# Starting the merge's first product one tile at a time, with the last gate chunk and the turning of the attention outputs moved around it

## The chip, the cores and the metric

The kernel runs on one core of a Trainium2 chip, as one launch. The metric is the time of a launch in device microseconds (us); the number used is the median of several runs. The engines are named as in the profile: PE is TensorE's matmul pipe and PEld its weight loads, DVE is VectorE, ACT is ScalarE, POOL is GpSimd and SP is SyncE, which issues most DMAs.

## The reference, cut to what matters

The model is two layers of FFN, token mixing and FFN, then one hybrid layer with attention and a mixture of experts. Sequence 256, width 1024, fp32. The change touches the end of the attention and the start of what follows it, the merge:

```python
# token_mix, each of the two layers; o_a and o_b are 256x512
g_a, g_b = jnp.split(g_merge, 2, axis=-1)
y = jax.nn.sigmoid(g_a) * (o_a @ w_branch_a) + jax.nn.sigmoid(g_b) * (o_b @ w_branch_b)
return y @ w_out
# hybrid_layer, once; y_a comes from a convolution, y_b from attention
merged = jax.nn.sigmoid(gate_conv_l) * p_a + jax.nn.sigmoid(gate_attn_l) * p_b
x = x + gate1[:, None, :] * (merged @ w_o)
```

## The kernel before

Every weight is streamed from HBM in blocks of 128x2048 fp32 (1 MB), three blocks to a unit. SP loads block r of the next unit into `raw` once DVE has taken the old one apart (`load_stream`, L421). ACT rounds each block to `w_hi` in two halves (`split`, L506) when it has landed and PE has freed the place (`used`); DVE then writes the rest, `w_lo` (L945). Every large product is three matmuls (`mm3`, L1754 to L1756): high times high, low times high, high times low. Activations that are a left operand are split the same way after PE has turned (transposed) them into PSUM.

The order of the work is written out by hand, a list for each engine, and each engine takes its own list strictly in order; semaphores hold the lists together. In the attention, `jobs_run` walks 12 jobs in each of the two layers (`JOBS`) and 4 in the hybrid layer (`HYB_JOBS`). A job is one kind of attention, one tile of 128 queries and 4 heads. In step j PE issues the scores of job j+1, then `beside(j)`, then the turning of job j's probabilities (L1995, behind ACT's four Exp of that job, L614), then P times V of job j-1 (L1977). PV of the last job comes behind the loop. ACT copies the turned probabilities out (L624) and DVE scales each P times V output into `o_a`, `o_b` or `o_h` (`job_out`, L1202 and L1212), which gives PSUM bank 6 free for the next P times V (`o_done`).

`beside(j)` holds work that has nothing to do with the attention. On PE it is a chunk of the product for the merge's gates: two or three of 24 row blocks of the four gate sets in the layers, half a set in the hybrid layer, into banks 2 and 3. On ACT it is the `w_hi` half of a block split, and, where a set is finished, its two Sigmoids out of banks 2 and 3 (L729, hybrid L761). On DVE it is the `w_lo` half of that split.

Behind the jobs PE turns the outputs `o_a` and `o_b` (two groups of 4 transposes each, L2005), ACT rounds them (L738), DVE takes the rest (L1428). In the hybrid layer only `o_h`, the right-hand product's operand, is turned here (ACT L826, DVE L1564); the left-hand one comes from the convolution and is there earlier. Then `merge`: the first half is the product with the first branch's weights, 4 chunks for each of two token tiles, tile 0 into banks 0 and 1, tile 1 into banks 2 and 3 (`half_product`); a tile ends with a one-column matmul (`release`, L1735) which tells DVE that it is done. DVE multiplies it by the gate (L1150, `ya_done`), and the second half, with the second branch's weights into the same banks, waits for that tile by tile. The merge uses three weight units: the first half reads blocks 0 and 1 of the first, the second half block 2 of it and block 0 of the next.

```python
jobs_run(l * NJ, l * 6, JOBS, beside)                       # PE, L2165
pe.wait_ge(w_evac_a, l * 9 + 9)
pe.wait_ge(o_done, l * NJ + NJ)
for b in range(4):
    o = o_a if b < 2 else o_b
    ...
merge(u_mix + MIX_IN_UNITS, l, True)
```

## Time and profile before

| what | us |
|---|---|
| median of 3 runs | 1853.35 |
| lowest and highest of them | 1852.48, 1854.16 |
| the profiled execution's own time | 1855.78 |
| its span in the profile | 1854.1 |

| engine | busy us | share of the span |
|---|---|---|
| PE | 1764.3 | 95% |
| PEld | 1427.1 | 77% |
| DVE | 1376.3 | 74% |
| ACT | 957.9 | 52% |
| POOL | 46.9 | 3% |

Busy time on PE is the sum of pipelined matmuls and says only where it stood still, not that it ran at its peak. The chain that ended last is followed back from the last instruction; its shares say which engine set the time. All times below are us from the start of the span, in the one profiled execution.

### The profile page before, as it was taken

To read this page: it belongs to the slowest core of one execution; us is meant where nothing else is said; L and a number is where in the kernel's file an instruction comes from. 1 tells how busy PE (TensorE), PEld (TensorE's weight loads), DVE (VectorE), ACT (ScalarE), POOL (GpSimd) and SP (SyncE) were. 2 spreads that over 40 slices of the span, in tenths; PEclk is the share of its full clock that TensorE was granted. 3 is DMA by queue.
4 is the path that set the end of the run, shared out by engine and by line. 5 is a ranking of instruction groups with operands and counts; after the bars stand their busy time and mean duration, and the time that the engine had idled before them with its cause. 6 is when DMAs were issued, how large, how long until landed. Compare 5 with 4: busy or idle time off the path is not lost.

```text
span 1854.1 us, 24899 instructions
## 1 busy us (share of the span) xinstructions
PE 1764.3 (95%) x8645; PEld 1427.1 (77%) x8645; DVE 1376.3 (74%) x2097; ACT 957.9 (52%) x1433; POOL 46.9 (3%) x92
## 2 busy tenths in 40 slices
PE   5999999999999999999999999999899897999998
PEld 3788778787788878886878777887687775888876
DVE  6887676766876578777677578775776477999997
ACT  3444354664544454445437554444434546777775
POOL 0000000000000000000000000000000000000000
PEclk8999999999999999999989999999998998999999
DMA  8988743134576758884612338986562533999994
GB/s 361 359 324 301 287 172 136 69 127 169 204 280 257 255 187 336 316 305 174 248 69 92 135 138 311 343 302 245 189 253 93 203 136 114 363 347 375 347 350 166
DMA packets 61802, 437.43 MB, mean 236 GB/s; under 512 B 6816, under 2 KB 7328, under 8 KB 9504
## 3 DMA queue, kind: packets, MB, share of 16 engines
q1 hardware_dynamic: 47504, 339.27, 48.6%
q0 software_dynamic: 12672, 92.28, 13.4%
q10 hardware_dynamic: 1552, 4.89, 0.8%
q8 instruction: 47, 0.77, 0.2%
q14 instruction: 27, 0.22, 0.0%
HBM read 435.36 MB, written 1.05 MB: 235 GB/s over the span
## 4 chain that ended last, share of the span: by engine, by line
PE 82%; DVE 11%; ACT 4%; issue 2%; DMA 1%; ACTq 0%; SPq 0%; DVEq 0%; POOLq 0%
PE bank L1754 24%; PE bank L1755 24%; PE bank L1756 24%; DVE w_lo L945 2%; PE bank L1977 2%; DVE ada_w L969 1%; ACT w_hi L506 1%; PE bank L1995 1%; DMA ada_w<-ada_pairs 1%; PE bank L1836 1%; PE bank L1957 1%; DVE arena L1243 1%; PE bank L2005 1%; PE bank L1955 1%; PE bank L2297 1%
## 5 line engine op out<-in xcount | busy, mean ns | idle before, releaser
L945 DVE TENSOR_TENSOR w_lo<-raw,w_hi 128x1024 fp32r<-128x1024 f32 x426 | 501.5, 1220 | 223.2 <-ACT w_hi L506 222.9
L506 ACT ACTIVATE w_hi<-raw 128x1024 fp32r<-128x1024 f32 x426 | 426.5, 1053 | 363.3 <-PE bank L1756 359.2
L1754 PE MATMUL bank<-w_hi,uT_hi 128*128 128x512 f32 (+3 forms) x1424 | 558.4, 392 | 20.3 <-DVE uT_lo L1260 12.6
L1755 PE MATMUL bank<-w_lo,uT_hi 128*128 128x512 f32 (+3 forms) x1424 | 543.9, 382 | 0.0
L1756 PE MATMUL bank<-w_hi,uT_lo 128*128 128x512 f32 (+3 forms) x1424 | 543.4, 382 | 0.0
L1754 PEld LDWEIGHTS bank<-w_hi,uT_hi 128*128 128x128 f32 x1424 | 271.5, 191 | 80.1 <-DVE uT_lo L1260 14.0
L1756 PEld LDWEIGHTS bank<-w_hi,uT_lo 128*128 128x128 f32 x1424 | 270.7, 190 | 52.1
L1755 PEld LDWEIGHTS bank<-w_lo,uT_hi 128*128 128x128 f32 x1424 | 271.6, 191 | 48.6 <-issue 1.4
L1754 PE MATMUL bank<-w_hi,r_arena 128*128 128x512 f32 (+1 forms) x744 | 299.1, 402 | 6.2 <-DVE r_arena L1652 2.3
L1755 PE MATMUL bank<-w_lo,r_arena 128*128 128x512 f32 (+1 forms) x744 | 295.1, 397 | 0.0
L1756 PE MATMUL bank<-w_hi,r_arena 128*128 128x512 f32 (+1 forms) x744 | 292.6, 393 | 0.0
L969 DVE CUSTOM_DVE_ANT_0 ada_w<-ada_w,cmpw 128x1024 f32<-128x1024 f32 x176 | 206.9, 1218 | 5.9 <-DMA ada_w<-ada_pairs 5.9
L1754 PEld LDWEIGHTS bank<-w_hi,r_arena 128*128 128x128 f32 x744 | 140.8, 189 | 42.0 <-DVE r_arena L1652 3.0
L1756 PEld LDWEIGHTS bank<-w_hi,r_arena 128*128 128x128 f32 x744 | 140.4, 189 | 32.9
L1755 PEld LDWEIGHTS bank<-w_lo,r_arena 128*128 128x128 f32 x744 | 140.8, 189 | 30.1
L952 DVE TENSOR_TENSOR w_lo<-raw,w_hi 128x1024 fp32r<-128x1024 f32 x94 | 110.8, 1221 | 10.4 <-ACT w_hi L514 10.3
L514 ACT ACTIVATE w_hi<-raw 128x1024 fp32r<-128x1024 f32 x94 | 94.1, 1052 | 15.2 <-PE bank L1756 15.2
L556 ACT ACTIVATE arena<-bank 128x256 f32<-128x256 f32 x88 | 33.8, 385 | 121.8 <-PE bank L1756 121.8
L476 POOL DMA_DIRECT2D ada_w<-ada_pairs x88 | 46.7, 530 | 1321.7 <-DVE mods_gate L969 572.4
L952 DVE TENSOR_TENSOR w_lo<-ada_w,w_hi 128x1024 fp32r<-128x1024 f32 x64 | 75.2, 1220 | 5.7 <-ACT w_hi L514 4.8
L514 ACT ACTIVATE w_hi<-ada_w 128x1024 fp32r<-128x1024 f32 x64 | 64.1, 1054 | 8.3 <-PE bank L1756 8.3
L614 ACT ACTIVATE arena<-arena,stat 128x256 f32<-128x256 f32 (+1 forms) x112 | 49.4, 444 | 23.6 <-DVE stat L1195 23.5
(328 smaller groups left out, 1470.6 us busy)
## 6 DMA issues: line engine op xcount, KB each, us to landing
raw<-weight_stream SPq DMA_DIRECT2D x216, 1024.0 KB, 4.9
ada_w<-ada_pairs POOLq DMA_DIRECT2D x88, 1024.0 KB, 5.2
raw<-expert_blocks SPq DMA_DIRECT2D x48, 1024.0 KB, 4.8
ada_w<-expert_blocks SPq DMA_DIRECT2D x32, 1024.0 KB, 4.9
cmpw<-expert_blocks SPq DMA_DIRECT2D x16, 1024.0 KB, 4.8
arena<-ada_pairs SPq DMA_DIRECT2D x5, 1024.0 KB, 13.8
ada_w<-ada_pairs SPq DMA_DIRECT2D x3, 1024.0 KB, 13.8
cmpw<-compress_w ACTq DMA_DIRECT2D x2, 1024.0 KB, 8.7
```

Source lines behind the costliest of these rows:

```text
L476: pool.dma_start(ada_w[:, slot], ada[g]).then_inc(ada_landed[slot], 16)
L506: act.activation(w_hi[:, b], v, ACT.Copy).then_inc(hi_done, 1)
L514: act.activation(w_hi[:, b], v, ACT.Copy).then_inc(hi_done, 1)
L556: act.activation(act_g[:, t], GU[t][:, 0:F_UNIT], ACT.Silu).then_inc(silu_done, 1)
L614: e = act.activation(v, v, ACT.Exp, bias=nmax[j % 2][:, h:h + 1], accum_out=psum_row[j % 4][:, h:h + 1])
L945: V.tensor_tensor(w_lo[:, b], v, f32(w_hi[:, b]), ALU.subtract).then_inc(split_done, 1)
L952: V.tensor_tensor(w_lo[:, b], v, f32(w_hi[:, b]), ALU.subtract).then_inc(split_done, 1)
L969: e = V.tensor_tensor_reduce(w[:, i], w[:, i], c, 1.0, 0.0, ALU.mult, ALU.add, dst[:, i:i + 1])
L1754: pe.matmul(dst, xh, w_hi[:, off:off + n], start=first, stop=False, skip_group_check=True)
L1755: pe.matmul(dst, xh, w_lo[:, off:off + n], start=False, stop=False, skip_group_check=True)
L1756: return pe.matmul(dst, xl, w_hi[:, off:off + n], start=False, stop=last, skip_group_check=True)
L1977: m = pe.matmul(HT[:, a * DH:(a + 1) * DH], pT[j % 2][:, kt, a], v, start=kt == 0, stop=kt == qt, skip_group_check=True)
```

## The change

On all engines `beside` of the last job moves behind everything of the last loop step, so that the last gate chunk stands ahead of the last P times V alone. An `ending` is called ahead of it. In the two layers that ending is the turning of `o_a` (banks 0 and 1 now, in place of 3 and 4) with its rounding on ACT and its rest on DVE. The merge's first half is cut in two calls, `merge_begin` for tile 0 directly behind the last P times V, then the turning of `o_b` (or `o_h`), then tile 1, whose banks 2 and 3 need the Sigmoids done. In the hybrid layer ACT takes a block's `w_hi` ahead of the last Sigmoids in place of behind them.

```diff
         HYB_JOBS = [(3, qt, g) for qt in (1, 0) for g in (0, 1)]
         NJ = len(JOBS)
+        O_BANKS = (0, 1, 5, 6)
...
-            def jobs_run(j0, jobs, beside=lambda j: None):
+            def jobs_run(j0, jobs, beside=lambda j: None, ending=lambda: None):
                 job_exp(j0, jobs, 0)
                 for j, (kind, qt, g) in enumerate(jobs):
-                    beside(j)
+                    if j + 1 < len(jobs):
+                        beside(j)
                     act.wait_ge(pt_psum, j0 + j + 1)
...
                     if j + 1 < len(jobs):
                         job_exp(j0, jobs, j + 1)
+                ending()
+                beside(len(jobs) - 1)
...
-                jobs_run(l * NJ, JOBS, beside)
+                def o_turned(bs):
+                    for b in bs:
+                        act.wait_ge(oT_psum, l * 4 + b + 1)
+                        act.activation(oT_hi[b // 2][:, 2 * (b % 2):2 * (b % 2) + 2], bank[O_BANKS[b]][:, :].rearrange("p (c s) -> p c s", c=2),
+                                       ACT.Copy).then_inc(oT_hi_done, 1)
+
+                jobs_run(l * NJ, JOBS, beside, ending=lambda: o_turned((0, 1)))
                 act.dma_start(c_bc, c_rows[0]).then_inc(c_landed, 16)
                 act.dma_start(c_next, c_rows[l]).then_inc(c_landed, 16)
...
+                o_turned((2, 3))
                 merge(u_mix + MIX_IN_UNITS, l)
...
                 else:
+                    split(um, (1,))
                     hyb_gates(3)
-                    split(um, (1,))
...
                     if j + 1 < len(jobs):
                         job_bias(j0, jobs, j + 1)
-                    beside(j)
+                        beside(j)
...
                     if j:
                         job_out(j0, jobs, j - 1)
+                ending()
+                beside(len(jobs) - 1)
                 job_out(j0, jobs, len(jobs) - 1)
...
+                jobs_run(l * NJ, JOBS, beside, ending=lambda: o_turned((0, 1)))
+                o_turned((2, 3))
                 dve.wait_ge(w_evac_a, l * 9 + 9)
...
+            def merge_begin(u0, m, t):
+                half_product((oT_hi[0], oT_lo[0]), [(u0, k * D) for k in range(4)], {1: 0, 3: 1}, [(oT_ready, 4 * m + 2)] * T, pa_psum, tiles=(t,))
+
             def merge(u0, m, close2):
                 u1, u2 = u0 + 1, u0 + 2
-                half_product((oT_hi[0], oT_lo[0]), [(u0, k * D) for k in range(4)], {1: 0, 3: 1}, [(oT_ready, 4 * m + 2)] * T, pa_psum)
                 pe.wait_ge(oT_ready, 4 * m + 4)
...
                     if j:
                         pv_job(j0, jobs, j - 1, v0 + nv if jobs[j - 1][1] else None)
                     nv += qt
+                ending()
+                beside(len(jobs) - 1)
                 pv_job(j0, jobs, len(jobs) - 1, v0 + nv if jobs[-1][1] else None)
...
+                jobs_run(l * NJ, l * 6, JOBS, beside, ending=lambda: turn_o((0, 1)))
+                merge_begin(u_mix + MIX_IN_UNITS, l, 0)
+                pe.wait_ge(o_done, l * NJ + NJ)
+                turn_o((2, 3))
                 pe.wait_ge(w_evac_a, l * 9 + 9)
-                pe.wait_ge(o_done, l * NJ + NJ)
...
+                merge_begin(u_mix + MIX_IN_UNITS, l, 1)
                 merge(u_mix + MIX_IN_UNITS, l, True)
...
             um = u + HYB_IN_UNITS
+            merge_begin(um, DEPTH, 0)
             pe.wait_ge(o_done, DEPTH * NJ + len(HYB_JOBS))
...
+            pe.wait_ge(w_evac_a, DEPTH * 9 + 13)
+            merge_begin(um, DEPTH, 1)
             merge(um, DEPTH, False)
```

PE's list in the first layer, from the P times V of job 9 on, before the change. `bank4<-cst,arena` is the turning of probabilities, `bank6<-arena` P times V, `w_hi,uT_hi` a gate product, `bank3<-cst,arena` the turning of an output, `w_hi,r_arena` the merge:

```order
L1977 MATMUL bank6<-arena 128x64 x7
L1754 MATMUL bank2<-w_hi,uT_hi 128x512 [waits blocks_split]
...
L1735 MATMUL bank7<-zeros 128x1
L1995 MATMUL bank4<-cst,arena 128x128 [waits pt_copied_v,pt_copied_a,exp_done]
L1995 MATMUL bank4<-cst,arena 128x128 x3
L1977 MATMUL bank6<-arena 128x64 [waits o_done,pt_copied_a]
...
L2005 MATMUL bank3<-cst,arena 128x128 [waits o_done,w_evac_a]
...
L1754 MATMUL bank0<-w_hi,r_arena 128x512 [waits blocks_split,oT_ready]
```

The same stretch of the changed kernel:

```order
L1991 MATMUL bank6<-arena 128x64 x7
L2009 MATMUL bank4<-cst,arena 128x128 [waits pt_copied_v,pt_copied_a,exp_done]
...
L2021 MATMUL bank0<-cst,arena 128x128 x4
L2021 MATMUL bank1<-cst,arena 128x128 x4
L1766 MATMUL bank2<-w_hi,uT_hi 128x512 [waits blocks_split]
...
L1747 MATMUL bank7<-zeros 128x1
L1991 MATMUL bank6<-arena 128x64 [waits o_done,pt_copied_a]
...
L1766 MATMUL bank0<-w_hi,r_arena 128x512 [waits blocks_split,oT_ready]
...
L2021 MATMUL bank5<-cst,arena 128x128 [waits o_done]
```

The last probabilities are turned, job 10's P times V is made and `o_a` is turned ahead of the gate chunk's 12 matmuls; one P times V is left behind them, and half of the output turning now stands between the merge's two tiles.

DVE's list at the same place, before (`bank6,stat` scales a P times V output, `w_lo<-raw,w_hi` is the split beside the last job, `r_arena<-bank3` the rest of a turned output):

```order
L1212 TENSOR_TENSOR arena<-bank6,stat 128x2x64
L945 TENSOR_TENSOR w_lo<-raw,w_hi 128x1024 [waits blocks_hi] x2
...
L1202 RECIPROCAL stat<-stat 128x4 [waits pv_done]
...
L1428 TENSOR_TENSOR r_arena<-bank3,r_arena 128x512 [waits oT_hi_done]
...
L945 TENSOR_TENSOR w_lo<-raw,w_hi 128x1024 [waits blocks_hi,w_evac_a]
```

And changed:

```order
L1219 TENSOR_TENSOR arena<-bank6,stat 128x2x64 [waits vector_chain]
...
L1437 TENSOR_TENSOR r_arena<-bank0,r_arena 128x512 [waits oT_hi_done]
L1437 TENSOR_TENSOR r_arena<-bank1,r_arena 128x512 [waits oT_hi_done]
L952 TENSOR_TENSOR w_lo<-raw,w_hi 128x1024 [waits blocks_hi] x2
L1209 RECIPROCAL stat<-stat 128x4 [waits pv_done]
...
L1437 TENSOR_TENSOR r_arena<-bank5,r_arena 128x512 [waits oT_hi_done]
L1437 TENSOR_TENSOR r_arena<-bank6,r_arena 128x512 [waits oT_hi_done]
L952 TENSOR_TENSOR w_lo<-raw,w_hi 128x1024 [waits blocks_hi,w_evac_a]
```

The split now stands behind the first two rests, and the other two rests stand behind the last output's scaling with the wait for PE's second turning between them; the split of the merge's third block is queued behind those.

## Rows read from the trace of the kernel before

**Rows 1.** the page, the chain that ended last: share of the span by engine
```profile
PE 82%; DVE 11%; ACT 4%; issue 2%; DMA 1%; ACTq 0%; SPq 0%; DVEq 0%; POOLq 0%
```

**Rows 2.** timeline of PE, first layer, 407 to 430: start, us, engine, line, op
```profile
407.95 0.48 PE L1754 MATMUL bank<-w_hi,uT_hi 128*128 128x512 f32 x1
...
410.85 0.63 PE L1995 MATMUL bank<-cst,arena 128*128 128x128 f32 x4
...
413.42 1.10 PE L1977 MATMUL bank<-arena 128*128 128x64 f32 x8 [1.10 <-ACT arena L624]
...
415.41 1.94 PE L2005 MATMUL bank<-cst,arena 128*128 128x128 f32 x16 [0.89 <-DVE arena L1212]
...
418.05 0.49 PE L1754 MATMUL bank<-w_hi,r_arena 128*128 128x512 f32 x1 [0.70 <-DVE r_arena L1428]
...
423.75 0.18 PE L1735 MATMUL bank<-zeros 128*128 128x1 bf16 x1
...
429.49 0.18 PE L1735 MATMUL bank<-zeros 128*128 128x1 bf16 x1
```

**Rows 3.** timeline of ACT, the same stretch
```profile
408.39 0.19 ACT L614 ACTIVATION_READ_ACCUMULATOR arena<-arena,stat 128x1 f32 x1
...
408.48 2.00 ACT L506 ACTIVATE w_hi<-raw 128x1024 fp32r<-128x1024 f32 x2
...
410.50 1.28 ACT L729 ACT_TABLE_LOAD   x1
...
412.76 0.60 ACT L624 ACTIVATE arena<-bank 128x512 f32<-128x512 f32 x1
...
416.07 2.06 ACT L738 ACTIVATE r_arena<-bank 128x512 fp32r<-128x512 f32 x4 [2.71 <-PE bank L2005]
...
418.00 2.03 ACT L506 ACTIVATE w_hi<-raw 128x1024 fp32r<-128x1024 f32 x2
```

**Rows 4.** timeline of DVE, the same stretch
```profile
416.70 2.48 DVE L1428 TENSOR_TENSOR r_arena<-bank,r_arena 128x512 fp32r<-128x512 f32 x4 [1.44 <-ACT r_arena L738]
...
419.18 2.36 DVE L945 TENSOR_TENSOR w_lo<-raw,w_hi 128x1024 fp32r<-128x1024 f32 x2
...
423.97 1.28 DVE L1150 TENSOR_TENSOR arena<-arena,bank 128x512 f32<-128x512 f32 x2 [2.42 <-PE bank L1735]
```

**Rows 5.** timeline of PE, second layer
```profile
1049.63 0.51 PE L1754 MATMUL bank<-w_hi,r_arena 128*128 128x512 f32 x1 [0.70 <-DVE r_arena L1428]
```

**Rows 6.** timeline of PE, hybrid layer, 1457 to 1486
```profile
1457.99 0.48 PE L1754 MATMUL bank<-w_hi,uT_hi 128*128 128x512 f32 x1
...
1463.56 0.60 PE L1995 MATMUL bank<-cst,arena 128*128 128x128 f32 x4
...
1468.94 1.94 PE L1977 MATMUL bank<-arena 128*128 128x64 f32 x8 [3.94 <-DVE arena L1212]
...
1471.67 1.97 PE L2005 MATMUL bank<-cst,arena 128*128 128x128 f32 x8 [0.79 <-DVE arena L1212]
...
1473.29 0.78 PE L1754 MATMUL bank<-w_hi,r_arena 128*128 128x512 f32 x1
...
1485.60 0.18 PE L1735 MATMUL bank<-zeros 128*128 128x1 bf16 x1
```

**Rows 7.** timeline of ACT, hybrid layer
```profile
1458.42 0.19 ACT L614 ACTIVATION_READ_ACCUMULATOR arena<-arena,stat 128x1 f32 x1
...
1464.73 2.00 ACT L506 ACTIVATE w_hi<-raw 128x1024 fp32r<-128x1024 f32 x2
```

**Rows 8.** timeline of DVE, hybrid layer
```profile
1465.82 2.36 DVE L945 TENSOR_TENSOR w_lo<-raw,w_hi 128x1024 fp32r<-128x1024 f32 x2 [6.90 <-ACT w_hi L506]
```

**Rows 9.** windows: span, us, busy by engine, granted clock, DMA share, GB/s
```profile
413.00:418.05 5.05, 3.04 (x25) 2.70 (x25) 2.07 (x7) 2.34 (x6) 0.00 (x0) 1.00 0.95 397
...
1469.00:1472.00 3.00, 2.21 (x10) 2.02 (x11) 0.67 (x3) 0.00 (x0) 0.00 (x0) 0.50 0.79 276
```

**Rows 10.** SP's weight loads, 395 to 475
```profile
DMA to landing us min/median/max: 4.8/4.8/6.7
```

More of the change, by code:

```diff
@@ L730, in beside @@
                         e.then_inc(w_evac_a, 1)
-                jobs_run(l * NJ, JOBS, beside)
+                def o_turned(bs):
[4 more added lines that the diff above has]
+                jobs_run(l * NJ, JOBS, beside, ending=lambda: o_turned((0, 1)))
                 act.dma_start(c_bc, c_rows[0]).then_inc(c_landed, 16)
                 act.dma_start(c_next, c_rows[l]).then_inc(c_landed, 16)
-                for b in range(4):
-                    act.wait_ge(oT_psum, l * 4 + b + 1)
-                    act.activation(oT_hi[b // 2][:, 2 * (b % 2):2 * (b % 2) + 2], bank[3 + b][:, :].rearrange("p (c s) -> p c s", c=2),
-                                   ACT.Copy).then_inc(oT_hi_done, 1)
+                o_turned((2, 3))
                 merge(u_mix + MIX_IN_UNITS, l)
@@ L1222, in job_out, with jobs_run @@
                     link(e)
-            def jobs_run(j0, jobs, beside=lambda j: None):
+            def jobs_run(j0, jobs, beside=lambda j: None, ending=lambda: None):
                 job_bias(j0, jobs, 0)
@@ L1423, in beside, with o_turned @@
                         split(u_mix + m, (b,))
-                jobs_run(l * NJ, JOBS, beside)
-                for b in range(4):
-                    dve.wait_ge(oT_hi_done, l * 4 + b + 1)
-                    V.tensor_tensor(oT_lo[b // 2][:, 2 * (b % 2):2 * (b % 2) + 2], bank[3 + b][:, :].rearrange("p (c s) -> p c s", c=2),
-                                    f32(oT_hi[b // 2][:, 2 * (b % 2):2 * (b % 2) + 2]), ALU.subtract).then_inc(oT_ready, 1)
+                def o_turned(bs):
+                    for b in bs:
+                        dve.wait_ge(oT_hi_done, l * 4 + b + 1)
+                        V.tensor_tensor(oT_lo[b // 2][:, 2 * (b % 2):2 * (b % 2) + 2], bank[O_BANKS[b]][:, :].rearrange("p (c s) -> p c s", c=2),
+                                        f32(oT_hi[b // 2][:, 2 * (b % 2):2 * (b % 2) + 2]), ALU.subtract).then_inc(oT_ready, 1)
+                jobs_run(l * NJ, JOBS, beside, ending=lambda: o_turned((0, 1)))
+                o_turned((2, 3))
                 dve.wait_ge(w_evac_a, l * 9 + 9)
@@ L1887, in ffn, with half_product @@
                 down(u0 + n - 1, f0 + n - 1, last=True)
-            def half_product(lhs, chunks, closes, ready, done, late=lambda: None):
+            def half_product(lhs, chunks, closes, ready, done, late=lambda: None, tiles=range(T)):
                 seen = {}
-                for t in range(T):
+                for t in tiles:
                     pe.wait_ge(*ready[t])
@@ L1978, in pv_job, with jobs_run @@
                 m.then_inc(pv_done, 1)
-            def jobs_run(j0, v0, jobs, beside=lambda j: None, first=lambda: None):
+            def jobs_run(j0, v0, jobs, beside=lambda j: None, first=lambda: None, ending=lambda: None):
                 nv = 0
@@ L1986, in jobs_run @@
                         sc_job(j0, jobs, j + 1)
-                    beside(j)
+                        beside(j)
                     pe.wait_ge(exp_done, j0 + j + 1)
@@ L2163, in beside, with turn_o @@
                             release(w_done)
-                jobs_run(l * NJ, l * 6, JOBS, beside)
-                pe.wait_ge(w_evac_a, l * 9 + 9)
-                pe.wait_ge(o_done, l * NJ + NJ)
-                for b in range(4):
-                    o = o_a if b < 2 else o_b
-                    for i in range(2):
-                        c = 2 * (b % 2) + i
-                        m = turn_rows(bank[3 + b][:, i * S:i * S + S], lambda t, c_: o[:, t, c_], slice(c * P, c * P + P))
-                    m.then_inc(oT_psum, 1)
+                def turn_o(bs):
+                    for b in bs:
+                        o = o_a if b < 2 else o_b
+                        for i in range(2):
+                            c = 2 * (b % 2) + i
+                            m = turn_rows(bank[O_BANKS[b]][:, i * S:i * S + S], lambda t, c_: o[:, t, c_], slice(c * P, c * P + P))
+                        m.then_inc(oT_psum, 1)
+                jobs_run(l * NJ, l * 6, JOBS, beside, ending=lambda: turn_o((0, 1)))
+                merge_begin(u_mix + MIX_IN_UNITS, l, 0)
+                pe.wait_ge(o_done, l * NJ + NJ)
+                turn_o((2, 3))
+                pe.wait_ge(w_evac_a, l * 9 + 9)
+                merge_begin(u_mix + MIX_IN_UNITS, l, 1)
                 merge(u_mix + MIX_IN_UNITS, l, True)
```

## The prediction

> **What bounds the kernel.** I began with the chain that ended last [rows 1]: 82% of the span is PE, so a microsecond in which PE stands still is a microsecond of the kernel, unless it is made up later, and a wait of DVE or ACT costs only where PE waits for it. Then the timeline of PE where the attention hands over to the merge [rows 2], the timelines of ACT and DVE beside it [rows 3, 4], the same place in the second layer [rows 5] and in the hybrid layer [rows 6 to 8].
>
> In the first layer the reader should see three pauses of PE in a row [rows 2]: 1.10 us ahead of the last P times V, for ACT's copy of the probabilities; 0.89 ahead of the turning of the outputs, for DVE's scaling; 0.70 ahead of the merge, for the rest of the turned outputs. Together 2.69 us. The first comes from ACT's order [rows 3]: the last Exp ended at 408.58, then came a split, the table load at 410.50, both Sigmoids, and only at 412.76 the copy. The second layer repeats it: its merge begins at 1049.63, also after 0.70 of idle time [rows 5], and the work around it is the same.
>
> In the hybrid layer the pause ahead of the last P times V is 3.94 us [rows 6]: bank 6 is given free by a scaling that DVE had queued behind a split begun at 1465.82 [rows 8], and that waited for ACT, which had the split behind the Sigmoids and began it at 1464.73 [rows 7]. Another 0.79 follows. Behind the long pause the granted clock was 0.50 from 1469 to 1472, the 1.2 GHz level, and in the first layer's stretch 1.00, the 2.4 GHz level, though PE was busy for only 3.04 of 5.05 us [rows 9].
>
> **The change in a layer.** I call PE free at 407.95, where the gate chunk began [rows 2], and lay its new list end to end.
> - New wait: the last probabilities can be turned only after the last Exp, at 408.39 + 0.19 = 408.58 [rows 3]. With 0.07 for the semaphore (ACT's copy ended at 413.36 and PE went on at 413.42 [rows 2, 3]) PE stands from 407.95 to 408.65: 0.70. Its bounds are 0, if PE's list hides it, and 1.1, the largest pause in these rows.
> - The turning of the probabilities to the next matmul takes 0.47, job 10's P times V 1.0, the turning of `o_a` half of 1.94, and the gate chunk from 407.95 to 410.85, 2.90 [rows 2]. None of it is new work, so only waits count.
> - The last P times V, behind the gates, needs the copy and job 10's scaling. Both now have 1.0 + 2.9 us of PE's work over them, the copy takes 0.60 [rows 3] and the scaling 0.89 [rows 2]. The pause of 1.10 goes.
> - The merge's tile 0 needs `o_a` alone. Rounding starts 0.66 behind the start of the turning (415.41 and 416.07), and the rest of two tiles ends 2.6 behind it (416.70 plus half of 2.48) [rows 2 to 4]; over it lie the turning, 2.90 of gates and 1.10 of P times V, 5.0. The pause of 0.70 goes, with 2.4 to spare.
> - Tile 0 runs directly behind the last P times V, so the scaling (0.89) lies under its 5.70 (418.05 to 423.75) [rows 2]. The second pause goes too.
> - Half the turning now splits the two tiles. [...]
> - The weights. The block that tile 0 needs for its third chunk is the one split beside the last job. ACT takes it behind the two roundings, at about 411.9, DVE is done with it near 415.3; PE reaches tile 0 at about 415.0 and its third chunk at 417.8. Nothing, with 2.5 to spare. If that cover were gone PE would wait in tile 0. SP reloads the slot some 3.4 us later; a load lands after 4.8, at most 6.7 [rows 10], and ACT wants it only when tile 1 is over, near 427.5. Nothing.
> - The Sigmoids end near 416.2 in place of 412.9; tile 1 wants their banks at about 421.8. Nothing. ACT's two small DMAs, behind them, are wanted in the next norm.
>
> So a layer gains 2.69 - 0.70 - 0.1 = 1.9 us, both layers 3.8.
>
> **The tight place.** ACT and DVE take their lists in order, and both stop at `o_b`'s turning, with the third block's split and tile 0's gate product queued behind it on DVE. Let that turning start at S. ACT rounds until S + 1.75 and then takes the block's halves; the first is there at S + 2.75, DVE's split (2.36) ends at S + 5.15, the gate product (1.28) at S + 6.45 [rows 3, 4]. PE turns for 1.0 and runs tile 1 for 5.74 (423.75 to 429.49) [rows 2], so it asks for this product at S + 6.75. The margin is 0.3 us. I cost the wait at nothing, and keep up to 1.5 us at each of three places for the range.
>
> **The change in the hybrid layer.** From 1457.99 to 1485.60 PE took 27.61 [rows 6]. Now: wait for the last Exp, 1458.42 + 0.19 + 0.07 - 1457.99 = 0.69 [rows 6, 7]; probabilities 0.43 to 0.47; P times V 1.0; gates 1463.56 - 1457.99 = 5.57 [rows 6]; P times V 1.10, tile 0 5.70, tile 1 5.74 at the first layer's prices, which had the full clock [rows 2]; turning 1.0. The sum is 21.3, the gain 6.3. In it are the pauses of 3.94 and 0.79, less 0.69, and what the low clock took: P times V 1.94 against 1.10, both tiles 12.31 (1473.29 to 1485.60) against 11.44, and some 0.6 in the turning, 2.3 in all [rows 2, 6]. The long pause goes twice over: the scaling is ahead of the split on DVE, and the split ahead of the Sigmoids on ACT. The weights landed long before, since ACT did not wait at 1464.73 [rows 7].
>
> The rows show the low level behind a 3.94 us pause and not behind pauses of about 1 us [rows 6, 9]. The Trainium skill's "TensorE: Matmul & The Clock Gate" (section "A second HAM failure mode: psum-queue depth-cycling") speaks against a list like the new one: short idles between groups of matmuls that go through PSUM banks can make the clock swing between its levels. By that page the small groups packed ahead of the gates would be at risk; by the window from 413 to 418 [rows 9] they are not, and the sum goes by the row.
>
> **Sum.** 3.8 + 6.3 = 10.1 us. Everything behind the merges follows events and not a fixed time, so I expect the shift to reach the end. The profiled execution's own time, 1855.78, becomes 1845.7. It stood 2.4 above the median of the runs; 1853.35 less 10.1 is **1843.2 us**, -0.55%.
>
> **Rivals.**
> - DVE is late at the second half. For it: the margin of 0.3 at the end of a chain of 6.45, whose every link is read in another order. Against it: the next steps have room, since DVE stood idle for 2.42 before its first gate product [rows 4]. At 1.1 us in each of three merges: 1843.2 + 3.3 = 1846.5.
> - The reordering does not do what it says in the layers, because tile 0, begun early, stops at its third chunk for the block split late. It needs ACT or DVE to be 2.5 us later than laid out. With a wait of 1.9 there a layer gains nothing and 1847.0 is left.
> - The clock falls where small groups are packed. The hybrid layer's loss of 2.3 at each of three places, taken off: 1843.2 + 6.9 = 1850.1, no change.
> - Slower: the weight stream runs behind. SP reloads a slot only after DVE's split, and these splits move back by some 4 us at the merge's first two blocks. Each block that then lands after ACT wants it delays PE, ACT and the next reload in turn. It decides once landing takes more than about 12 us (the 7 us of slack plus 4.8), and to end over 1857 it must cost (10.1 + 3.7) / 3 = 4.6 us a merge, a landing near 17 us. The longest one here took 6.7 [rows 10].
>
> **How the numbers follow.** My forecast 0.77, late DVE 0.13, late block 0.04, clock 0.04, weight stream 0.02. The low end takes the Exp wait and the split turning as nothing: 3 x 0.7 + 0.2 = 2.3 less, about 1840.8. The high end takes in the late DVE and the late block: 1847.0. A measurement of this kernel can tell about 0.2%, 3.7 us, from no change. Faster by more than that hold the first three, 0.94; within it the clock, 0.04; slower the weight stream, 0.02.
>
> **What would show it.** In the changed profile PE should run from the new wait of about 0.7 to the end of tile 1 without a pause over 0.3, in all three places; the hybrid layer's granted clock should stay 1.00; the last P times V there should take about 1.0 and not 1.94; tile 1 should end near 427.5 in the first layer. A pause of PE at the first matmul of the second half, released by the gate product on DVE, would be the first rival; one inside tile 0, released by DVE's split, the second. If the waits go as told and the time does not, a later stage takes it back, and the forecast is wrong there.

## The result, and the profile after

The changed kernel took 1840.43 us (median of 5 runs, 1837.27 to 1841.68), the kernel before 1852.48 beside it (5 runs, 1848.82 to 1854.16): a ratio of 0.993, 95% interval 0.9918 to 0.9942, faster by 12.1 us. The profiled execution took 1840.43, its span is 1838.8.

Busy time by engine, and the chain that ended last:

```profile
PE 1760.5 (96%) x8645; PEld 1423.5 (77%) x8645; DVE 1375.7 (75%) x2097; ACT 958.5 (52%) x1433; POOL 46.9 (3%) x92
...
PE 84%; DVE 10%; ACT 3%; DMA 1%; issue 1%; ACTq 0%; SPq 0%; DVEq 0%; POOLq 0%
```

The work is the same (8645 matmuls), and PE's share of the chain went from 82 to 84% [rows 1]. The timeline of PE in the first layer, from the P times V of job 9 to the second half (start, us, engine, line, op):

```profile
401.83 1.90 PE L1991 MATMUL bank<-arena 128*128 128x64 f32 x16
404.21 0.66 PE L2009 MATMUL bank<-cst,arena 128*128 128x128 f32 x4 [0.49 <-ACT arena L615]
404.71 1.00 PE L1991 MATMUL bank<-arena 128*128 128x64 f32 x8
405.55 1.04 PE L2021 MATMUL bank<-cst,arena 128*128 128x128 f32 x8
406.35 0.48 PE L1766 MATMUL bank<-w_hi,uT_hi 128*128 128x512 f32 x1
...
409.20 0.18 PE L1747 MATMUL bank<-zeros 128*128 128x1 bf16 x1
409.24 1.08 PE L1991 MATMUL bank<-arena 128*128 128x64 f32 x8
410.14 0.47 PE L1766 MATMUL bank<-w_hi,r_arena 128*128 128x512 f32 x1
...
415.82 0.18 PE L1747 MATMUL bank<-zeros 128*128 128x1 bf16 x1
415.86 1.07 PE L2021 MATMUL bank<-cst,arena 128*128 128x128 f32 x8
416.69 0.48 PE L1766 MATMUL bank<-w_hi,r_arena 128*128 128x512 f32 x1
...
422.37 0.18 PE L1747 MATMUL bank<-zeros 128*128 128x1 bf16 x1
422.41 0.49 PE L1766 MATMUL bank<-w_hi,r_arena 128*128 128x512 f32 x1
```

The three pauses of [rows 2] are gone. One is left, the new wait for the last Exp, in brackets at 404.21. DVE in the same stretch:

```profile
417.16 1.29 DVE L1437 TENSOR_TENSOR r_arena<-bank,r_arena 128x512 fp32r<-128x512 f32 x2 [5.93 <-ACT r_arena L740]
418.67 2.36 DVE L952 TENSOR_TENSOR w_lo<-raw,w_hi 128x1024 fp32r<-128x1024 f32 x2 [0.22 <-ACT w_hi L507]
420.95 1.28 DVE L1157 TENSOR_TENSOR arena<-arena,bank 128x512 f32<-128x512 f32 x2
```

Here is the tight place of the prediction: the gate product that PE's second half wants ended at 420.95 + 1.28 = 422.23, PE asked for it at 422.41. And the hybrid layer, PE:

```profile
1447.51 1.90 PE L1991 MATMUL bank<-arena 128*128 128x64 f32 x16
1449.89 0.66 PE L2009 MATMUL bank<-cst,arena 128*128 128x128 f32 x4 [0.48 <-ACT arena L615]
1450.39 1.00 PE L1991 MATMUL bank<-arena 128*128 128x64 f32 x8
...
1456.77 1.00 PE L1991 MATMUL bank<-arena 128*128 128x64 f32 x8
1457.58 0.48 PE L1766 MATMUL bank<-w_hi,r_arena 128*128 128x512 f32 x1
...
1463.31 1.07 PE L2021 MATMUL bank<-cst,arena 128*128 128x128 f32 x8
```

and its window, with the columns of [rows 9]:

```profile
1448.00:1470.00 22.00, 21.52 (x116) 17.84 (x116) 9.52 (x18) 11.70 (x21) 0.00 (x0) 1.00 0.69 280
```

The window's columns are the busy times of PE, PEld, DVE, ACT and POOL, the granted clock, the DMA share and GB/s. The pause of 3.94 us and the low clock behind it [rows 6, 9] are both gone: P times V takes 1.00 where it took 1.94, and the granted clock is 1.00 throughout.

To compare kernels I measure in each trace one stretch, called the place from here on: from the start of job 9's P times V (of job 1's in the hybrid layer) to the end of the merge's tile 1, that is to its one-column matmul. Everything that the change moves on PE lies inside. The starts before, in layer 1 and in the hybrid layer, and the end in the changed hybrid layer, which no rows above show:

```profile
406.25 1.90 PE L1977 MATMUL bank<-arena 128*128 128x64 f32 x16
...
1456.28 1.90 PE L1977 MATMUL bank<-arena 128*128 128x64 f32 x16
```

```profile
1469.83 0.18 PE L1747 MATMUL bank<-zeros 128*128 128x1 bf16 x1
```

| | layer 1 | layer 2 | hybrid | sum |
|---|---|---|---|---|
| before | 406.25 to 429.49, 23.24 | 23.23 | 1456.28 to 1485.60, 29.32 | 75.79 |
| after | 401.83 to 422.37, 20.54 | 20.54 | 1447.51 to 1469.83, 22.32 | 63.40 |
| gain | 2.70 | 2.69 | 7.00 | 12.4 |

The two spans differ by 15.3 us, so 2.9 lie outside. The place in layer 1 starts 4.42 earlier, behind code that the change doesn't touch. Between places 1 and 2 it is 0.99 less, between 2 and 3 2.03 more, behind place 3 0.47 more. Over the 14 profiles of this study the start lies between 399.1 and 406.3, the stretch between places 1 and 2 takes 605.0 to 611.4, that between 2 and 3 393.6 to 400.4, and what lies behind place 3 368.3 to 369.6. The four differences are inside these spreads, so I put none of them down to the change; for the 0.47 at the end that isn't shown. The medians differ by 12.1, near the places' 12.4. So I judge every experiment by its places, and the medians stand beside them.

### The profile page after: what moved, and what is told of

Read it like the earlier page. It is cut to its first block, busy times and chain, and to the rows that moved or that the text cites. A ratio compares the mean times of both kernels' runs of the same rounds, so it can differ in the third digit from the quotient of the medians.

```text
span 1838.8 us, 24900 instructions
## 1 busy us (share of the span) xinstructions
PE 1760.5 (96%) x8645; PEld 1423.5 (77%) x8645; DVE 1375.7 (75%) x2097; ACT 958.5 (52%) x1433; POOL 46.9 (3%) x92
## 4 chain that ended last, share of the span: by engine, by line
PE 84%; DVE 10%; ACT 3%; DMA 1%; issue 1%; ACTq 0%; SPq 0%; DVEq 0%; POOLq 0%
PE bank L1766 25%; PE bank L1767 24%; PE bank L1768 24%; DVE w_lo L952 2%; PE bank L1991 2%; DVE ada_w L976 1%; PE bank L2009 1%; DMA ada_w<-ada_pairs 1%; PE bank L1848 1%; ACT w_hi L507 1%; PE bank L2021 1%; PE bank L1971 1%; DVE arena L1252 1%; PE bank L2321 1%; PE bank L1969 1%
## 5 line engine op out<-in xcount | busy, mean ns | idle before, releaser
L1766 PE MATMUL bank<-w_hi,uT_hi 128*128 128x512 f32 (+3 forms) x1424 | 557.9, 392 | 18.9 <-DVE uT_lo L1269 11.1
L1768 PE MATMUL bank<-w_hi,uT_lo 128*128 128x512 f32 (+3 forms) x1424 | 543.5, 382 | 0.0
L1766 PEld LDWEIGHTS bank<-w_hi,uT_hi 128*128 128x128 f32 x1424 | 271.2, 190 | 79.1 <-DVE uT_lo L1269 13.1
L1768 PEld LDWEIGHTS bank<-w_hi,uT_lo 128*128 128x128 f32 x1424 | 270.7, 190 | 52.0
L1766 PE MATMUL bank<-w_hi,r_arena 128*128 128x512 f32 (+1 forms) x744 | 297.9, 400 | 4.8 <-DVE r_arena L1664 2.3
L1768 PE MATMUL bank<-w_hi,r_arena 128*128 128x512 f32 (+1 forms) x744 | 292.5, 393 | 0.0
L1766 PEld LDWEIGHTS bank<-w_hi,r_arena 128*128 128x128 f32 x744 | 140.2, 188 | 40.0 <-DVE r_arena L1664 3.0
L1768 PEld LDWEIGHTS bank<-w_hi,r_arena 128*128 128x128 f32 x744 | 140.1, 188 | 32.8
```

Source lines behind the costliest of these rows:

```text
L1766: pe.matmul(dst, xh, w_hi[:, off:off + n], start=first, stop=False, skip_group_check=True)
L1768: return pe.matmul(dst, xl, w_hi[:, off:off + n], start=False, stop=last, skip_group_check=True)
```

## The experiments

Two theories to begin with. Mine: each pause is its own, what is moved gains what its pause cost, and in the hybrid layer the clock follows the pause. The rival: the pauses' cost is not the idle time that the profile prints, or it returns elsewhere; for the clock, that something other than a long pause lowers it. All numbers are us; a ratio is against runs of the kernel before on the same chip.

| kernel | layer 1 | layer 2 | hybrid | median (lowest to highest, runs) | ratio, 95% |
|---|---|---|---|---|---|
| layers_only | 20.52 | 20.52 | 30.22 | 1846.31 (1844.72 to 1853.77, 10) | 0.9969, 0.9956 to 0.9981 |
| split_first | 23.23 | 23.23 | 25.30 | 1848.79 (1843.85 to 1851.85, 7) | 0.9977, 0.9963 to 0.9990 |
| split_first_again | 23.24 | 23.23 | 25.29 | 1853.28 (1 run) | |
| warm | 23.24 | 23.24 | 26.81 | 1850.12 (1846.83 to 1856.69, 10) | 0.9985, 0.9970 to 1.0000 |
| tiles_together | 21.73 | 21.73 | 23.33 | 1842.97 (1841.41 to 1846.21, 4) | 0.9943, 0.9927 to 0.9960 |
| gates_only | 22.56 | 22.56 | 23.33 | 1843.03 (1841.36 to 1845.12, 5) | 0.9946, 0.9923 to 0.9969 |
| turn_twice | 21.39 | 21.39 | 22.32 | 1840.19 (1839.57 to 1843.69, 4) | 0.9937, 0.9913 to 0.9961 |
| dve_late | 20.54 | 20.55 | 22.32 | 1843.14 (1840.86 to 1848.01, 8) | 0.9951, 0.9936 to 0.9967 |
| dve_later | 20.54 | 20.54 | 22.32 | 1840.19 (1 run) | |
| fill_wait | 19.92 | 19.92 | 21.67 | 1839.49 (1836.87 to 1847.58, 6) | 0.9936, 0.9912 to 0.9959 |
| fill_again | 19.92 | 19.93 | 21.67 | 1840.01 (1837.01 to 1843.56, 6) | 0.9922, 0.9900 to 0.9944 |
| changed_again | 20.52 | 20.52 | 22.32 | 1841.23 (1839.05 to 1845.39, 6) | 0.9936, 0.9913 to 0.9958 |

By time alone the kernels of this table with more than one run fall into two loose groups, with medians of 1839.5 to 1843.1 and of 1846.3 to 1850.1; inside a group the intervals overlap, and warm's reaches 1. What tells the kernels apart are the places.

**1. The layers alone.** The changed kernel with its hybrid layer as before, on every engine:

```diff
-            def jobs_run(j0, jobs, beside=lambda j: None, ending=lambda: None):
+            def jobs_run(j0, jobs, beside=lambda j: None, ending=lambda: None, late=True):
...
-                    if j + 1 < len(jobs):
+                    if j + 1 < len(jobs) or not late:
                         beside(j)
...
+                    hyb_gates(3)
                     split(um, (1,))
-                    hyb_gates(3)
...
-            merge_begin(um, DEPTH, 0)
             pe.wait_ge(o_done, DEPTH * NJ + len(HYB_JOBS))
...
             pe.wait_ge(w_evac_a, DEPTH * 9 + 13)
+            merge_begin(um, DEPTH, 0)
             merge_begin(um, DEPTH, 1)
```

> The changed kernel with the hybrid layer's part undone. Theory (the gain is made at the three places alone and adds up: 2.7 us in each layer, 7.0 in the hybrid layer): from the turning of the last-but-one job's probabilities to the end of tile 1, 20.97 us in each of the two layers as in the changed kernel, 29.75 in the hybrid layer as before; about 5.4 us under the kernel before, some 1847. Rival (a good part of the 12 us comes from elsewhere, such as the start of the run): the time stays near the changed kernel's, 1841 to 1843, though the hybrid stretch is long again.

(The 20.97 and 29.75 count from the turning ahead of the place, some 0.43 earlier; by the place they are 20.54 and 29.32.) The layers keep their gain, 2.72 and 2.71. The hybrid place went from 29.32 to 30.22 with the same order of work. The pauses are the same, 3.94 and 0.80, but two windows of this run, against one of the kernel before, show a longer stretch at the low level. In layers_only tile 0 begins at 1469.55:

```profile
1470.00:1473.00 3.00, 3.00 (x8) 2.32 (x8) 2.52 (x4) 2.42 (x3) 0.00 (x0) 0.50 0.00 0
1473.00:1476.00 3.00, 3.00 (x13) 2.36 (x13) 0.94 (x1) 0.00 (x0) 0.00 (x0) 0.92 0.26 44
```

before, at 1473.29 [rows 6]:

```profile
1474.00:1477.00 3.00, 3.00 (x12) 2.39 (x11) 2.51 (x4) 2.16 (x3) 0.00 (x0) 0.79 0.00 0
```

A mean of 0.79 puts the rise near 1475.3, 2.0 us into tile 0; a mean of 0.92 near 1473.5, 3.9 us into it. Nearly 2 us more at half the clock is the 0.9. So what the long pause costs varies by that much between profiles, and with it the hybrid layer's gain: 7.0 against the one profile, 7.9 against the other. The layers' gain does not depend on it.

**2. ACT's order alone, in the hybrid layer.** The kernel before with one line moved:

```diff
-                    hyb_gates(3)
                     split(um, (1,))
+                    hyb_gates(3)
```

> The kernel before, with only ACT's split taken ahead of the last Sigmoids in the hybrid layer. Theory (the pause of 3.94 us is ACT's order, and the low clock follows from the pause): the pause ahead of the last P times V falls to about 0.8, the granted clock stays 1.00, and 3.1 + 2.3 = 5.4 us go. Rival one (the clock falls there for another reason): 3.1 us go. Rival two (P times V waited for something else): under 1 us goes.

PE's timeline, and two windows behind it:

```profile
1459.24 1.00 PE L1977 MATMUL bank<-arena 128*128 128x64 f32 x8
1461.13 1.08 PE L1977 MATMUL bank<-arena 128*128 128x64 f32 x8 [0.89 <-DVE arena L1212]
1463.00 1.20 PE L2005 MATMUL bank<-cst,arena 128*128 128x128 f32 x8 [0.80 <-DVE arena L1212]
```

```profile
1462.00:1463.00 1.00, 0.21 (x2) 0.07 (x2) 0.67 (x3) 0.00 (x0) 0.00 (x0) 1.00 0.99 418
1464.00:1465.00 1.00, 1.00 (x4) 0.81 (x4) 0.68 (x2) 1.00 (x3) 0.00 (x0) 0.50 0.99 418
```

The mechanism holds: with the split ahead of the Sigmoids the pause falls from 3.94 to 0.89, and the last P times V starts 1.89 behind the one before it, not 4.95. But the place gained 4.0, not 5.4. The clock still fell, to 0.50 from about 1464 to 1467, behind pauses of 0.89 and 0.80; there the matmuls started 0.43 apart, not 0.23. Both tiles took 12.98 (1463.85 to 1476.83), where the first layer's took 11.44 at the full clock [rows 2]: 1.5 more, about the 1.4 that was missed.

**3. The same kernel once more**, to see whether that low clock was chance.

> The kernel before with ACT's split ahead of the last Sigmoids, profiled a second time. The first time the granted clock fell to 0.50 from about 1463.9 on though PE's longest pause was 0.89 us. Theory (whether the clock falls there depends on where the execution stands in time as well as on the pauses): the pauses are 0.89 and 0.80 again, and the low stretch may be shorter, longer or absent; the place takes from 24.3 us (no low clock) to 25.3. Rival (the pattern of pauses alone decides): 25.3 again with the same low stretch.

The place took 25.29, and behind the same two pauses the low level was there again:

```profile
1470.00:1472.00 2.00, 2.00 (x6) 1.53 (x5) 1.72 (x3) 2.00 (x4) 0.00 (x0) 0.50 0.99 422
```

So it was there in both profiles of this kernel, and the rival's 25.3 came true. (The 24.3 named for no low clock is too high: 25.30 less the 1.5 is 23.8.) Yet three pauses in a row of 1.10, 0.89 and 0.70 in the layers left the clock at 1.00 [rows 2, 9]. What decides between the two places isn't settled.

**4. The pause kept, the clock held.** The kernel before, with 15 matmuls of zeros, whose result nobody reads, in the long pause:

```diff
+                if len(jobs) < NJ:
+                    keep_warm(15, SPARE[:, 0:512])
                 pv_job(j0, jobs, len(jobs) - 1, v0 + nv if jobs[-1][1] else None)
```

> The kernel before, with 15 matmuls on zeros put into the hybrid layer's pause of 3.94 us, 3.2 us of them at the full clock. Theory (the low clock is the price of PE standing still): P times V starts when it did, takes 1.0 in place of 1.94, the turning and the merge's first matmuls run at the full clock, 2.3 us go. Rival (the clock would fall anyway): nothing goes, 1852.5, and the window around the last P times V shows 0.50 again.

```profile
1462.29 3.19 PE L1744 MATMUL bank<-zeros 128*128 128x512 bf16 x14
...
1466.17 1.08 PE L1977 MATMUL bank<-arena 128*128 128x64 f32 x8 [0.70 <-DVE arena L1212]
1468.05 1.09 PE L2007 MATMUL bank<-cst,arena 128*128 128x128 f32 x8 [0.80 <-DVE arena L1212]
```

(The trace has 14 of the 15.) The window from 1466 to 1469 has the clock at 1.00, P times V takes 1.08 in place of 1.94, and the place gained 2.51 where 2.3 were named as the low clock's cost. So that part of the hybrid layer's gain is the clock, and 7.00 less 2.51, 4.5 us, is waiting. Against the 30.22 of layers_only, the same list with a longer low stretch, the clock's part would be 3.4. The median, 1850.12 with an interval up to 1.0000, doesn't tell this kernel from the one before; the 2.51 is the place's.

**5. The outputs turned ahead of both tiles.** The changed kernel, with its `turn_o((2, 3))` and the hybrid layer's turning ahead of tile 0:

```diff
-                merge_begin(u_mix + MIX_IN_UNITS, l, 0)
                 pe.wait_ge(o_done, l * NJ + NJ)
                 turn_o((2, 3))
+                merge_begin(u_mix + MIX_IN_UNITS, l, 0)
```

> The changed kernel with both turnings ahead of tile 0 (the second output still has to wait for the last scaling). Theory (tile 0 is the cover of the scaling): a pause of 0.8 to 0.9 us comes back ahead of the second turning in all three places, 2.6 us above the changed kernel, some 1843. Rival (the split of the tiles brings nothing, since DVE's tight chain at the second half takes it back): the same time as the changed kernel, 1840.4.

```profile
411.94 1.08 PE L1991 MATMUL bank<-arena 128*128 128x64 f32 x8
414.00 1.09 PE L2021 MATMUL bank<-cst,arena 128*128 128x128 f32 x8 [0.97 <-DVE arena L1219]
```

The pause is back as expected, but it costs 1.19 a layer and 1.01 in the hybrid layer, 3.4 in all where 2.6 was expected. The printed idle time is 0.97; the starts are 2.06 apart, and 0.90 where nothing waits (409.24 to 410.14 in the changed kernel), which is 1.16 more. Here the sum by idle times failed, and a sum by starts, made afterwards, held to 0.03.

**6. The gate chunk alone.** The changed kernel without its `ending`, with all outputs turned together, in the hybrid layer too. PE's part in the layers; ACT's and DVE's lists follow it:

```diff
-                jobs_run(l * NJ, l * 6, JOBS, beside, ending=lambda: turn_o((0, 1)))
+                jobs_run(l * NJ, l * 6, JOBS, beside)
+                pe.wait_ge(o_done, l * NJ + NJ)
+                turn_o((0, 1, 2, 3))
                 merge_begin(u_mix + MIX_IN_UNITS, l, 0)
-                pe.wait_ge(o_done, l * NJ + NJ)
-                turn_o((2, 3))
...
```

> The changed kernel with its two other parts undone: only the last gate chunk is moved behind the last probabilities and job 10's P times V; all outputs are turned together behind the last P times V, and the tiles follow each other. From the start of job 9's P times V to the end of tile 1 it was 23.24 us in a layer before and 20.54 in the changed kernel. Theory (a wait costs PE what lies between the starts of two groups beyond the spacing they have when nothing waits, 0.84 for P times V): the move saves 2.10 - 0.84 = 1.26 and adds 0.67, so 22.65. Rival (a wait costs the idle time that the profile shows, 1.10): 22.84. Both: the hybrid stretch falls from 29.32 to 23.3, the pause of 3.94 gone and the one ahead of the turning left.

```profile
408.52 1.08 PE L1991 MATMUL bank<-arena 128*128 128x64 f32 x8
410.40 1.97 PE L2021 MATMUL bank<-cst,arena 128*128 128x128 f32 x16 [0.80 <-DVE arena L1219]
...
413.06 0.50 PE L1766 MATMUL bank<-w_hi,r_arena 128*128 128x512 f32 x1 [0.70 <-DVE r_arena L1437]
```

A layer takes 22.56, where the sum by starts had said 22.65 and the one by idle times 22.84. The 0.09 that is left is mostly the pause behind the last P times V, 1.88 from start to start (408.52 to 410.40) in place of 1.99. The edit of the gates alone gives 0.68 of a layer's 2.70, of which 1.26 - 0.67 = 0.59 is the pause ahead of P times V less the new wait; the rest, 2.02, comes of turning `o_a` early and running tile 0 ahead of `o_b`'s turning. In the hybrid layer the gates' move and ACT's order give 6.0 of the 7.0, and the clock stayed at 1.00 behind pauses of 0.48 and 0.80.

**7. A turning doubled.** `o_a` is turned twice, into the same banks:

```diff
+                def turn_twice():
+                    for b in (0, 1):
+                        for i in range(2):
+                            c = 2 * b + i
+                            turn_rows(bank[O_BANKS[b]][:, i * S:i * S + S], lambda t, c_: o_a[:, t, c_], slice(c * P, c * P + P))
+                    turn_o((0, 1))
+
+                jobs_run(l * NJ, l * 6, JOBS, beside, ending=lambda: turn_twice())
```

> The changed kernel with o_a turned twice in each of the two layers (8 more transposes into the same banks, nothing waits between them). Theory (a group that is not waited for costs its start-to-start spacing, 0.80): the stretch in a layer goes from 20.54 to 21.34. Rival (it costs the busy time that the profile shows for such a group, 1.04): 21.58. The hybrid stretch stays 22.32.

A layer takes 21.39, so it adds 0.85, near the 0.80 between the starts of 405.55 and 406.35, and not the 1.04 that the group is busy.

**8. DVE late.** Two copies that nobody reads, ahead of the split that stands before the gate product; then, in a second kernel, four:

```diff
             def merge(u0, m, stage, gates, following, between, more=True):
+                V.tensor_copy(ytmp[:, 0, 0], gates[3][:, 0])
+                V.tensor_copy(ytmp[:, 0, 1], gates[3][:, 0])
                 split(u0, (2,))
```

> The changed kernel with two extra copies (128x512, about 0.64 us each, results unused) on DVE ahead of the third block's split in each merge. Theory (DVE's chain from the second turning to tile 0's gate product ends only 0.1 to 0.3 us before PE asks for it): the second half's first tile, 5.74 us from end to end, takes 6.7 to 6.9 in all three merges, and the kernel 3.0 to 3.5 more, some 1843.5. Rival (DVE has room there): 5.74 again and 1840.4.

DVE and PE, two copies:

```profile
421.06 0.42 DVE L1153 COPY arena<-arena 128x512 f32<-128x512 f32 x1
...
424.00 1.28 DVE L1159 TENSOR_TENSOR arena<-arena,bank 128x512 f32<-128x512 f32 x2
```

```profile
425.07 0.18 PE L1749 MATMUL bank<-zeros 128*128 128x1 bf16 x1
425.38 0.47 PE L1768 MATMUL bank<-w_hi,r_arena 128*128 128x512 f32 x1
```

(The added source lines make L1749 and L1768 of the changed kernel's L1747 and L1766.) I had sized a copy by the operations with an operand in PSUM, 0.64. These read and write SBUF and start 0.34 apart. Measured from the start of PE's second turning, the gate product began 5.09 behind it in the changed kernel (415.86 to 420.95) and 5.44 here (418.56 to 424.00): DVE came 0.35 later. The second half's first tile took 5.99, 5.98 and 5.98 at the three places in place of 5.73, so 0.25 of the delay became PE's, which leaves a margin of 0.1. PE's next product stands 0.31 behind the release, in place of 0.04. By the places this costs 3 x 0.25 = 0.75 us; that the median, 1843.14, fell on the expected 1843.5 is chance. With four copies the delay was put to the test once more, by a sum with a delay of 0.45 and a margin of 0.2, which I had from the idle time printed ahead of the split, 0.22, and which are both 0.1 too high:

> The changed kernel with four extra copies of 0.34 us on DVE ahead of the third block's split in each merge, in place of the two of the run before, which delayed DVE by 0.45 and PE by 0.25. Theory (a margin of 0.2 us, and behind it PE pays one for one): 1.35 - 0.22 of idle time = 1.13 of delay, 0.93 for PE: 6.67 from end to end of the second half's first tile in all three merges. Rival (PE is caught by a looser chain): 5.99 again, or less than 6.3.

```profile
418.00 1.43 DVE L1154 COPY arena<-arena 128x512 f32<-128x512 f32 x4
...
421.61 1.28 DVE L1159 TENSOR_TENSOR arena<-arena,bank 128x512 f32<-128x512 f32 x2
```

```profile
422.00 0.18 PE L1749 MATMUL bank<-zeros 128*128 128x1 bf16 x1
422.98 0.48 PE L1768 MATMUL bank<-w_hi,r_arena 128*128 128x512 f32 x1 [0.80 <-issue]
```

The tile took 6.67, 6.68 and 6.66, as expected, because the two errors cancel: the gate product began 6.12 behind the turning (415.49 to 421.61), 1.03 later than in the changed kernel, and 0.94 of it is PE's, a margin of 0.1 again. The profile puts PE's wait down to "issue", but the gate product ended at 422.89 and PE went on 0.09 later, as it did with two copies (425.28 and 425.38). From two copies to four the delay grew by 0.68 and PE's tile by 0.69: past a margin of 0.1 a delay of DVE is PE's, one for one. The first rival's mechanism is real, the changed kernel just doesn't set it off. The places end ahead of it and kept their length. The one run took 1840.19, though its merges are 2.8 us longer, so a single time can't be read for such differences.

**9. The new wait filled.** Three matmuls of the last gate chunk go ahead of the last probabilities' turning:

```diff
+                def filling():
+                    i, k = GATE_CHUNKS[NJ - 1][0]
+                    m, off = gate_place(i, k)
+                    need(u_mix + m, seen[m], off, 512)
+                    mm3(bank[2][:, :], uT_hi[:, k, tok(0)], uT_lo[:, k, tok(0)], off, 512, k == 0, k == KD - 1)
...
                         for t in range(T):
+                            if (j, i, k, t) == (NJ - 1, *GATE_CHUNKS[NJ - 1][0], 0):
+                                continue
...
                         beside(j)
+                    else:
+                        filling()
```

and the same in the hybrid layer with the first row block of its last chunk.

> The changed kernel with the last gate chunk's first three matmuls put into PE's wait for the last Exp, in all three places. Theory (a wait costs start against start, 0.67 here, and what lies behind has room): from job 9's P times V to the end of tile 1 19.87 us in place of 20.54 in a layer and 21.65 in place of 22.32 in the hybrid layer, 2.0 us in all. Rival one (it costs the 0.49 of idle time that the profile shows): 20.05 and 21.83. Rival two (the shorter chunk no longer covers rounding and the block's split): a pause of PE ahead of tile 0 or at its third chunk and 20.5 again.

```profile
402.90 1.90 PE L1991 MATMUL bank<-arena 128*128 128x64 f32 x16
404.61 0.48 PE L1766 MATMUL bank<-w_hi,uT_hi 128*128 128x512 f32 x1
...
405.82 1.00 PE L1991 MATMUL bank<-arena 128*128 128x64 f32 x8
```

The profile prints no pause of PE at the three places. The places take 19.92, 19.92 and 21.67, which is 0.62, 0.62 and 0.65 less than the changed kernel's: 1.9 us. The idle time printed at the wait, 0.49, would have given 20.05; the starts (401.83 to 404.21, 2.38, against 1.70 before the change, 406.25 to 407.95) give 0.68 and 19.86, nearer but 0.06 too much.

**10. Both once more, side by side.** 1.9 us is 0.1%, so the changed kernel and the filled one ran again on one chip.

> The changed kernel once more, beside the next one. Theory and rival alike: 20.54 us from job 9's P times V to the end of tile 1 in both layers and 22.3 in the hybrid layer; 0.993 to 0.994 of the kernel before, 12.4 us by the three places. What lies between the places may differ by 2 us and more from one execution to another.

> The changed kernel with three gate matmuls in the wait for the last Exp, timed beside the changed kernel. By the places it is 0.62 + 0.62 + 0.65 = 1.9 us shorter. Theory (everything behind shifts with it): a ratio to the kernel before that is lower than the changed kernel's by about 0.001, hardly to be told with five rounds. Rival (a later stage takes it back): the same places, and no difference in the mean over both sessions.

The places repeat to 0.02. The medians, 1841.23 and 1840.01, lie the right way round and 1.2 apart, with intervals that overlap (0.9936, 0.9913 to 0.9958, and 0.9922, 0.9900 to 0.9944). So by its traces the filled kernel is the shortest at the places, and by time it isn't told apart from the changed one.

## Why the prediction was right, and where it was wrong

The direction was right and so were the mechanisms, but for a sentence on the clock; the forecast of 1843.2 was 2.8 us too high, and the median lies 0.4 below the low end of the range. Of the 2.8, 0.9 is the starting point: I took 10.1 off 1853.35, and the runs of the kernel before beside the changed one had 1852.48. The rest is a gain of 12.1 where I had 10.1. With the other starting point the same range would reach down to some 1840.0, so that the median lies outside by 0.4 is in part chance; that the gain was sized too small is not, since the places show it in every profile.

Two rows of the kernel before are needed beside [rows 2, 6], the last P times V but one of the first layer and of the hybrid layer:

```profile
411.32 1.00 PE L1977 MATMUL bank<-arena 128*128 128x64 f32 x8
...
1463.99 1.00 PE L1977 MATMUL bank<-arena 128*128 128x64 f32 x8
```

By the prediction's own steps:

- *The three pauses of a layer go*: right, all three. **The failed step is their size, "Together 2.69 us"**, and with it "a layer gains 1.9". I read the idle times that the profile prints. By starts: P times V 10 to 11 took 2.10 before (411.32 to 413.42) and takes 0.84 where nothing waits, so 1.26 and not 1.10; P times V to turning 1.99 against 0.90, 1.09 and not 0.89; turning to merge 2.64 against 0.80 + 0.83, 1.01 and not 0.70. The sum is 3.36. The difference from 2.69 is the tail of each group: a group of 8 is shown busy for 1.00 to 1.10 and the next can start after 0.80 to 0.90, so the idle time starts to count too late: 0.16, 0.20 and 0.31 for the three. Experiments 5, 7 and 9 each put a number on it: 1.19 where 0.97 idle was printed, 0.85 where 1.04 busy was, 0.62 where 0.49 idle was; sums by starts gave 1.16, 0.80 and 0.68. The Trainium skill's "Perfetto Trace Analysis" (section "Tensor Engine Instruction (MATMUL, LD_WEIGHTS)") says that the end of a TensorE instruction is an estimate from its size and not observed; the 0.80 between starts against 1.04 busy is in line with that, but these runs can't tell a modelled end from two groups that overlap.
- *The new wait, 0.70*: right, 0.68 by starts. I had worked it out from when Exp ends, not from an idle time.
- *The turning in two groups, 0.1*: no run shows such a cost. The halves take 0.80 and 0.83 from start to start, 1.63 in all, less than the 1.94 that the whole group was busy before. A layer is then 3.36 - 0.67 = 2.69, and 2.70 and 2.69 were measured.
- *The hybrid layer, 6.3*: 7.0 by the same step. In the terms of that sum, two P times V at 1.0 and 1.10 and a turning at 1.0 are busy times; by starts they take 0.81, 0.81 and 0.83, 0.65 less. By waits and starts: 4.95 - 0.81, 2.73 - 0.81, 1.62 - 0.83 and 0.9 for both tiles at the low clock, less 0.68 of new wait, are 7.1. "What the low clock took, 2.3" measured 2.51 with the pause kept (experiment 4).
- *Sum, 10.1*: 12.4 at the places. 1852.48 less 12.4 is 1840.1, and 1840.43 was measured. The low end took only the new wait and the turning at nothing, and by its own sum it is 1840.9; the printed idle times had no bounds of their own, and that was the range's fault.
- *"The low level behind a 3.94 us pause and not behind pauses of about 1 us"*: too strong. It holds for the layers, and experiments 2 and 3 show the low level behind 0.89 and 0.80. In the changed kernel the forecast of 1.00 came true. The rule of the Trainium skill's "TensorE: Matmul & The Clock Gate", section "A second HAM failure mode: psum-queue depth-cycling", that short idles between groups can swing the clock, is not borne out in the changed kernel (1.00 from 1448 to 1470); in split_first the clock did fall behind short idles, so I dismissed the warning too easily. Whether those two pauses are the page's case isn't shown.
- *The tight place, margin 0.3, cost nothing*: right, with a margin of 0.1 (experiment 8). Of the difference 0.17 is again the turning, laid down with its busy 1.0 where it takes 0.83. *The block split late, the Sigmoids, the weights*: nothing, right; tile 0 ran its 24 matmuls without a pause. (The rest of the turned outputs ends 2.53 behind the start of the turning, not 2.6; nothing hangs on it.)
- *Tile 1 ends near 427.5*: at 422.37, or 426.8 with the 4.42 us by which this profile started earlier; the rest of the difference, 0.7, is the tails and the 0.1 above.
- *The rivals*: none came true. Late DVE is real past 0.1 us; the reordering did what it says; the clock held; the weight stream kept up, since PE waits for no weights at any of the places.

Left open: what decides whether two short pauses lower the clock, and how much of the 2.9 us outside the places would return over more profiles. Why the next group can start ahead of the printed end of the last one isn't shown either; only by how much.

## What to carry to other kernels

Cost a wait of TensorE from start to start, against the same pair of groups where nothing waits, and not by the idle time printed or the busy time of small groups: here that step alone left some 2 of 12.4 us out of the forecast. When an engine stands still for a chain over two others, look for independent work that can stand behind the start of that chain, and check the other engines' lists for what is queued ahead of the link (ACT's split behind two Sigmoids cost 3 us by itself). Then look at the next link that the moved engine will ask for, and test its margin by adding work until it shows.

## What the runs showed of the hardware that was not expected

- Eight 128x128 fp32 transposes are shown busy for 1.04 us and take 0.80 to 0.85 of PE's time between other groups; eight P times V matmuls of 64 columns are shown at 1.00 to 1.10 and take 0.81 to 0.90.
- The granted clock fell to 0.50 behind pauses of 0.89 and 0.80 us, in two profiles of two (about 3 us at the low level, 1.5 us lost), and stayed at 1.00 behind 1.10, 0.89 and 0.70 in the layers, behind 0.48 and 0.80 in gates_only's hybrid layer and behind 0.70 and 0.80 in warm's.
- Behind one and the same pause of 3.94 us the low level lasted until 2.0 us into tile 0 in one profile and 3.9 us into it in another, 0.9 us of difference.
- 15 matmuls of zeros in a pause of 3.94 us, bf16 and 512 columns wide (3.19 us in the trace), held the clock at 1.00 and were worth 2.51 us.
- A DVE copy of 128x512 fp32 from SBUF to SBUF took 0.34 us from start to start; the gate product, two instructions of the same size with one operand in PSUM, took 1.19 (420.95 to 422.14), 0.60 each.
